# A residual stream through PSUM: where the sum between two phases is kept while the next norm reads it

## The reference, cut to what matters

```
def rms_norm(x, g):
    xf = x.astype(jnp.float32)
    y = xf * lax.rsqrt(jnp.mean(xf * xf, axis=-1, keepdims=True) + EPS)
    return (y * g.astype(jnp.float32)).astype(x.dtype)

# first block, twice
h = rms_norm(x, g_mix_norm[l]);  x = x + mix @ w_out[l]
h = rms_norm(x, g_ffn_norm[l]);  x = x + (silu(h @ w_gate[l]) * (h @ w_up[l])) @ w_down[l]

# second block, i = 0 (short convolution) and i = 1 (dilated attention)
h = h + mixed(rmsnorm(h, norm_mix[i]))
h = h + squared_relu_mlp(rmsnorm(h, norm_mlp[i]))
ple_gate = jax.nn.sigmoid(rmsnorm(h, norm_ple[i]) @ ple_w_gate[i])
h = h + ple_gate * (p[i] @ ple_w_proj[i])
return rmsnorm(h, norm_final)
```

## Time and profile before

| | us |
|---|---|
| median of 3 runs | 2726.02 |
| the profiled execution, whole | 2725.45 |
| its span | 2723.6 |
| TensorE busy | 2619.7 |
| GpSimd busy | 1665.5 |
| VectorE busy | 1270.6 |
| ScalarE busy | 471.2 |

### The profile page before, as it was taken

The page is one execution under the profiler, slowest core; times in us unless marked ns, Lnnn a source line. Parts: engine busy times, 40 slices in busy tenths (PEclk is TensorE's granted clock), DMA queues, the critical chain, the costliest instruction groups (busy, mean ns, idle before and its releaser), DMA issues.

```text
span 2723.6 us, 31500 instructions
## 1 busy us (share of the span) xinstructions
PE 2619.7 (96%) x11906; PEld 2146.2 (79%) x11906; DVE 1270.6 (47%) x1678; ACT 471.2 (17%) x777; POOL 1665.5 (61%) x1113
## 2 busy tenths in 40 slices
PE   7889999999899999999999999999999999999997
PEld 6668888877578888787888887788788878888885
DVE  5755443046654440345740514983367246604326
ACT  3332111023421110100100102300310042100012
POOL 5526677664276676666776766676347625767763
PEclk9899999999899999999999999999999999999998
DMA  4102222231022222222222222222112212232221
GB/s 151 62 16 93 100 100 93 94 113 62 16 93 96 104 92 93 93 93 93 101 97 103 92 93 101 91 95 93 63 47 92 100 40 70 93 108 93 93 92 62
DMA packets 36891, 236.70 MB, mean 87 GB/s; under 512 B 4048, under 2 KB 5584, under 8 KB 9168
## 3 DMA queue, kind: packets, MB, share of 16 engines
q1 hardware_dynamic: 33456, 230.78, 24.2%
q10 hardware_dynamic: 3360, 4.85, 0.5%
HBM read 233.51 MB, written 2.10 MB: 87 GB/s over the span
## 4 chain that ended last, share of the span: by engine, by line
PE 88%; DVE 7%; issue 2%; ACT 2%; POOL 0%; DMA 0%; DVEq 0%; SPq 0%; POOLq 0%; ACTq 0%
PE psum L457 27%; PE psum L458 27%; PE psum L459 27%; PE psum L906 2%; DVE work L1289 2%; DVE x_low L1303 1%; PE psum L890 1%; PE psum L668 1%; PE psum L915 1%; PE psum L778 1%; PE psum L794 0%; PE psum L487 0%; DMA x_res<-in_x 0%; DVE rstd L1296 0%; DVE work L1409 0%
## 5 line engine op out<-in xcount | busy, mean ns | idle before, releaser
L399 POOL TENSOR_TENSOR w_low<-w_stage,w_high 128x512 fp32r<-128x512 f32 x864 | 1214.4, 1436 | 18.0
L395 POOL TENSOR_SCALAR w_high<-w_stage 128x2048 fp32r<-128x2048 f32 x216 | 420.0, 1944 | 1004.8 <-PE psum L459 993.4
L457 PE MATMUL psum<-x_high,w_high 128*128 128x512 f32 x1664 | 654.5, 393 | 23.8 <-DVE x_low L1303 22.3
L458 PE MATMUL psum<-x_low,w_high 128*128 128x512 f32 x1664 | 648.7, 390 | 0.0
L459 PE MATMUL psum<-x_high,w_low 128*128 128x512 f32 x1664 | 648.6, 390 | 0.0
L457 PEld LDWEIGHTS psum<-x_high,w_high 128*128 128x128 f32 x1664 | 313.1, 188 | 94.9 <-issue 19.4
L458 PEld LDWEIGHTS psum<-x_low,w_high 128*128 128x128 f32 x1664 | 313.2, 188 | 67.2 <-issue 2.2
L459 PEld LDWEIGHTS psum<-x_high,w_low 128*128 128x128 f32 x1664 | 313.0, 188 | 65.3
L1329 DVE TENSOR_TENSOR x_res<-psum,x_res 128x512 f32<-128x512 f32 x64 | 47.0, 735 | 416.2 <-PE psum L459 416.2
L457 PE MATMUL psum<-mlp_high,w_high 128*128 (+1 forms) x576 | 225.5, 391 | 2.9 <-DVE mlp_low L1395 2.9
L458 PE MATMUL psum<-mlp_low,w_high 128*128 (+1 forms) x576 | 225.1, 391 | 0.0
(11 more groups left out here) (257 smaller groups left out, 3534.6 us busy)
## 6 DMA issues: line engine op xcount, KB each, us to landing
w_stage<-in_wstream SPq DMA_DIRECT2D x216, 1024.0 KB, 4.9
x_res<-in_x SPq DMA_DIRECT2D x2, 1024.0 KB, 11.7
out_x<-attn_out SPq DMA_DIRECT2D x8, 256.0 KB, 2.1
inv_count_sb<-in_inv_count ACTq DMA_DIRECT2D x2, 512.0 KB, 8.7
ple_proj<-in_p ACTq DMA_DIRECT2D x2, 512.0 KB, 3.7
qk<-in_mask ACTq DMA_DIRECT2D x1, 576.0 KB, 3.9
w_spat<-in_spatial ACTq DMA_DIRECT2D x2, 256.0 KB, 5.3
diag_sb<-in_diag ACTq DMA_DIRECT2D x2, 256.0 KB, 9.4
```

The source lines that it names most:

```text
L395: pool.tensor_scalar(wh[:, s, :], stage[:, s, :], 1.0, 1.0, ALU.mult, ALU.mult).then_inc(high_written, 1)
L399: last = pool.tensor_tensor(wl[:, s, part], stage[:, s, part], wh[:, s, part].bitcast(F32), ALU.subtract)
L457: pe.matmul(out, wa, ra, start=start, stop=False)
L458: pe.matmul(out, wa, rb, start=False, stop=False)
```

## The change

In all borders but the last one the sum of bank and x is written back **into the PSUM bank**. A new semaphore `x_summed` tells ScalarE of it. ScalarE copies the bank to x and makes the high part from the bank (`keep_sum`); VectorE makes x_low from the bank (`low_of_sum`); when that is done ScalarE squares the bank in place (`square_sum`), and VectorE adds the square from there to the running sum (`accumulate_sum`). Only then is the bank released. VectorE's order becomes: add of tile m, low of tile m-1, square-add of tile m-2. The gate's chain of ple (scale, sigmoid, product, sum) stays in the bank too, with a new semaphore `gate_scaled`. Before the final norm the gate's sum still goes to x and the squares to SBUF. In front of attn the bank is read with a step of four; behind attn the bank is read in a row, and x, high, low and the running sum are addressed with a step of four.

```diff
--- before.py
+++ after.py
...
@@ -357,6 +361,14 @@
             if p.kind == "attn":
                 return by_class(dst, False), by_class(x[:, m, :], True)
             return dst, x[:, m, :]
+
+        def summed_tile(p, before, m):
+
+            if before.kind == "attn":
+                return by_class(ps[:, m, :], False), lambda dst: by_class(dst, True)
+            if p.kind == "attn":
+                return by_class(ps[:, m, :], True), lambda dst: by_class(dst, False)
+            return ps[:, m, :], lambda dst: dst
 
         block = ctx.enter_context(nc.Block())
 
@@ -980,18 +992,41 @@
                 added[0] += 1
                 reader[n % 2] = (squares_added, added[0])
 
-            def scale_tile(p, m):
-                dst, src = operand(p, high_of(p, m), m)
-                act.activation(dst, src, ACT.Copy, scale=gcol(p.gain + m)).then_inc(x_scaled, 1)
-
-            def open_norm(p, ready, first):
+            def open_norm(p, before, first_square):
 
                 for m in range(DT):
-                    act.wait_ge(*ready[m])
-                    if p.kind != "final" and (m >= first or p.kind != "attn"):
-                        scale_tile(p, m)
-                    if m >= first:
+                    act.wait_ge(*x_ready(p, before, m))
+                    if p.kind != "final":
+                        act.activation(xh[:, m, :], x[:, m, :], ACT.Copy, scale=gcol(p.gain + m)).then_inc(x_scaled, 1)
+                    if m >= first_square:
                         norm_square(p, m)
+
+            def keep_sum(p, before, m):
+
+                act.wait_ge(*x_ready(p, before, m))
+                src, order = summed_tile(p, before, m)
+                if before.kind == "attn":
+                    act.activation(by_class(x[:, m, :], True), src, ACT.Copy)
+                else:
+                    act.activation(x[:, m, :], ps[:, m, :], ACT.Copy)
+                act.activation(order(high_of(p, m)), src, ACT.Copy, scale=gcol(p.gain + m)).then_inc(x_scaled, 1)
+
+            def square_sum(p, m):
+
+                act.wait_ge(x_low, 8 * p.norm + m + 1)
+                act.activation(ps[:, m, :], ps[:, m, :], ACT.Square).then_inc(squares_ready, 1)
+                n = state["sq"]
+                state["sq"] += 1
+                added[0] += 1
+                reader[n % 2] = (squares_added, added[0])
+
+            def open_psum_norm(p, before):
+
+                for m in range(DT + 1):
+                    if m < DT:
+                        keep_sum(p, before, m)
+                    if m >= 1:
+                        square_sum(p, m - 1)
 
             def split_tile(dst, src, scale=1.0):
                 act.activation(dst, src, ACT.Copy, scale=scale).then_inc(split_high, 1)
...
@@ -1051,10 +1084,16 @@
                     act.wait_ge(slab_done, p.slab)
                     load(mask_landing, a["mask2"])
                 for m in range(DT):
-                    act.wait_ge(drained[m], p.drain[m] + (2 if m < 7 else 3))
-                    act.activation(W[:, m % 2, :], W[:, m % 2, :], ACT.Sigmoid).then_inc(act_fn, 1)
-                    if m >= 2:
-                        next_square(m - 2)
+                    act.wait_ge(gate_scaled, DT * p.layer + m + 1)
+                    act.activation(ps[:, m, :], ps[:, m, :], ACT.Sigmoid).then_inc(act_fn, 1)
+                    if following.kind == "final":
+                        if m >= 2:
+                            next_square(m - 2)
+                    else:
+                        if m >= 1:
+                            keep_sum(following, p, m - 1)
+                        if m >= 2:
+                            square_sum(following, m - 2)
 
             def mix_loads(p):
                 L = p.layer
...
@@ -1296,38 +1342,65 @@
                 dve.reciprocal(dst, W[:, ROOT, :]).then_inc(rstd_ready, 1)
                 dve.wait_ge(rstd_ready, state["sums"])
 
-            def low(p, m):
-                dve.wait_ge(x_scaled, 8 * p.norm + m + 1)
-                dst, src = operand(p, low_of(p, m), m)
-                high, _ = operand(p, high_of(p, m).bitcast(F32), m)
-                dve.scalar_tensor_tensor(out=dst, in0=src, scalar=gcol(p.gain + m), in1=high,
-                                         op0=ALU.mult, op1=ALU.subtract).then_inc(x_low, 1)
-
-            def open_norm(p, residual, first):
+            def open_norm(p, first):
 
                 for m in range(DT + 1):
-                    if m < DT and residual:
-                        residual(m)
                     if m >= 1:
-                        if p.kind != "final" and (m > first or p.kind != "attn"):
-                            low(p, m - 1)
+                        if p.kind != "final":
+                            dve.wait_ge(x_scaled, 8 * p.norm + m)
+                            dve.scalar_tensor_tensor(out=xl[:, m - 1, :], in0=x[:, m - 1, :], scalar=gcol(p.gain + m - 1),
+                                                     in1=xh[:, m - 1, :].bitcast(F32), op0=ALU.mult, op1=ALU.subtract) \
+                                .then_inc(x_low, 1)
                         if m > first:
                             accumulate(m == 1)
                 state["acc_sum"] = state["sums"] + 1
+                finish_norm(p)
+
+            def low_of_sum(p, before, m):
+
+                dve.wait_ge(x_scaled, 8 * p.norm + m + 1)
+                src, order = summed_tile(p, before, m)
+                dve.scalar_tensor_tensor(out=order(low_of(p, m)), in0=src, scalar=gcol(p.gain + m),
+                                         in1=order(high_of(p, m).bitcast(F32)), op0=ALU.mult, op1=ALU.subtract).then_inc(x_low, 1)
+
+            def accumulate_sum(p, before, m):
+
+                n, k = state["sq"], state["added"]
+                dve.wait_ge(squares_ready, n + 1)
+                src, order = summed_tile(p, before, m)
+                acc = order(W[:, ACC, :])
+                if m == 0:
+                    at_least(dve, summed, state["acc_sum"])
+                    dve.tensor_copy(acc, src).then_inc(squares_added, 1)
+                else:
+                    tt(acc, acc, src, ALU.add).then_inc(squares_added, 1)
+                dve.wait_ge(squares_added, k + 1)
+                dve.sem_inc(drained[m], 1)
+                state["sq"] += 1
+                state["added"] += 1
+
+            def open_psum_norm(p, before):
+
+                signals = last_results(before)
+                for m in range(DT + 2):
+                    if m < DT:
+                        dve.wait_ge(*signals[m])
+                        if before.kind == "attn":
+                            flat = by_class(ps[:, m, :], False)
+                            tt(flat, flat, by_class(x[:, m, :], True), ALU.add).then_inc(x_summed, 1)
+                        else:
+                            tt(ps[:, m, :], ps[:, m, :], x[:, m, :], ALU.add).then_inc(x_summed, 1)
+                    if 1 <= m <= DT:
+                        low_of_sum(p, before, m - 1)
+                    if m >= 2:
+                        accumulate_sum(p, before, m - 2)
+                state["acc_sum"] = state["sums"] + 1
                 if p.kind != "ple":
                     finish_norm(p)
 
             def finish_norm(p):
                 dve.wait_ge(drained[7], p.drain[7] + (2 if p.kind == "ple" else 1))
                 reciprocal(rstd[:])
-
-            def add_from_psum(p):
-                signals = last_results(p)
-                def residual(m):
-                    dve.wait_ge(*signals[m])
-                    src, dst = operand(p, ps[:, m, :], m)
-                    tt(dst, src, dst, ALU.add).then_inc(drained[m], 1)
-                return residual
 
             def ffn(p):
                 with dve.Fori(0, FFN_TILES // 2) as i:
@@ -1402,17 +1475,25 @@
                 for m in range(DT + 1):
                     if m < DT:
                         dve.wait_ge(*tile_end(run, m))
-                        tt(W[:, m % 2, :], ps[:, m, :], rstd[:], ALU.mult).then_inc(drained[m], 1)
+                        tt(ps[:, m, :], ps[:, m, :], rstd[:], ALU.mult).then_inc(gate_scaled, 1)
                     if m >= 1:
                         k = m - 1
                         dve.wait_ge(act_fn, fn0 + k + 1)
-                        step(tt(W[:, k % 2, :], W[:, k % 2, :], pj[:, k, :], ALU.mult))
-                        tt(x[:, k, :], x[:, k, :], W[:, k % 2, :], ALU.add).then_inc(x_updated, 1)
-                        dve.wait_ge(x_updated, DT * p.layer + k + 1)
-                    if 2 <= m < DT:
-                        if following.kind == "attn":
-                            low(following, m - 2)
-                        accumulate(m == 2)
+                        step(tt(ps[:, k, :], ps[:, k, :], pj[:, k, :], ALU.mult))
+                        if following.kind == "final":
+                            tt(x[:, k, :], ps[:, k, :], x[:, k, :], ALU.add).then_inc(x_updated, 1)
```

(47 more changed lines are left out.)

## The result

| | us |
|---|---|
| before, median of 4 runs beside the changed kernel | 2725.07 (2722.59 to 2730.25) |
| after, median of 4 runs | 2700.55 (2695.03 to 2703.81) |
| ratio, 95% interval | 0.9906 [0.9895, 0.9918] |
| profiled execution, before and after | 2725.45 and 2697.78 |

A forecast was written before the change was run, and what follows sets the result against it. TensorE is busy 96%, so only its gaps, from late VectorE operations with two SBUF inputs beside GpSimd's splits, can be won: 7.0 + 4.9 + 7.1 + 2.6 + 3.4 = 25.0 us, median 2701, range 2697 to 2714.

The forecast's parts named there:

- Borders to mix and conv: Down projection to mix and to conv: VectorE at 2.06 a tile leaves TensorE no wait, gain 3.55 + 3.49 = 7.0 us.
- ple projections: Down projection to ple, twice: gain 2.42 + 2.49 = 4.9 us; banks held until the square-add, closest cover 1.1 us.
- ple to attention: First attention slab after ple's gate: 18.13 falls to 10.98, gain 7.1 us, taking strided PSUM reads at 1.13.
- Rival C: Strided PSUM reads take 2 us: attention's part turns from +7.1 to -1.3, total 2710; chance 0.06.
- Writes to PSUM: VectorE or ScalarE operations writing PSUM, not shown in the trace: taken at 0.69 us, bounds 0.67 and 1.13.
- Rival A: PSUM writes or handovers cost some tenths, 0.85 an operation in all: total 2709 to 2713; chance 0.15.
- the estimate by the errata section of the Trainium skill: PSUM sources cost 0.06 us more per VectorE operation, making the summed gain 1.5 us smaller.
- Mix output projection: Both mix output projections: w_low wait falls from 3.25 to 1.9, gain 2.6 us, plus 3.4 or 0 from the clock.
- conv: Border after conv's output projection: only the last tile counts, nothing lost now and nothing after.
- The final norm: Behind the last matmul: same operations in the same order, GpSimd idle, gain 0.
- at the borders: Borders to mix and conv, to ple, and to attention together: 7.0 + 4.9 + 7.1 = 19.0 us.

The follow-up runs named there:

- experiment 3: Kernel before, all operands in SBUF, only VectorE's order changed (square-add one tile later): 2720.78 us, ratio 0.9981.
- experiment 1: Kernel before with GpSimd's low split of the weights cut to 32 of every 512 columns from the third slab on: 2686.88 us, ratio 0.9854.
- experiment 6: Changed kernel with one more VectorE operation a tile, a copy of the square, between square-add and bank release: 2717.98 us, ratio 0.9973.
- experiment 7: Changed kernel with ScalarE's new copy made twice per tile, not at the border behind attention: 2705.5 us, ratio 0.9931.
- experiments 5 and 9: 5: changed kernel, gate chain and norm before attention back in SBUF, 2703.96 us. 9: changed kernel, conv's chain also kept in PSUM banks, 2693.41 us.
- changed kernel's second profile: The changed kernel run again unaltered, on the chip of two later kernels: 2696.47 us, ratio 0.9897.

## Why the prediction was right, step by step

- *Borders to mix and conv*, forecast 3.55 + 3.49, measured 14.43 - 10.88 and 14.37 - 10.88, the same two numbers. VectorE's pace came out as worked. Its queue at the border to mix (start, duration, operation):

```profile
578.06 0.70 DVE L1392 TENSOR_TENSOR psum<-psum,x_res 128x512 f32<-128x512 f32 x1
578.67 0.74 DVE L1363 SCALAR_TENSOR_TENSOR x_low<-psum,cols_sb,x_high 128x512 fp32r<-128x512 f32 x1
579.33 0.68 DVE L1376 TENSOR_TENSOR work<-work,psum 128x512 f32<-128x512 f32 x1
...
580.15 0.70 DVE L1392 TENSOR_TENSOR psum<-psum,x_res 128x512 f32<-128x512 f32 x1
```

  From add to add 2.09, where the forecast had 2.06. The step from square-add to add, 0.82, is longer than the other two, since VectorE first waits for the square-add's end to release the bank; the forecast had no term for that. The cause was half stated: the new order alone would bring 3.3 of these 7.0 (experiment 3), and short durations alone all of them (experiment 1). The forecast's queues were run with both; the text named the durations only.
- *ple projections*, forecast 2.42 + 2.49, measured the same in TensorE's stretch, and 2.52 and 2.61 to the norm's sum, because the late first gate matmul went too (0.1 each). The cover was as thin as said: one more VectorE operation a tile turns it into a loss (experiment 6), and one more ScalarE operation costs 1.6 each (experiment 7).
- *ple to attention*, forecast 7.1, measured 7.25. The result held with a wrong size in it. I took 1.13 and 1.2 for strided reads of PSUM; the trace has 0.68 for ScalarE's (above) and, by form, for VectorE's:

```profile
L1363 DVE SCALAR_TENSOR_TENSOR attn_x_low<-psum,cols_sb,attn_x_high 128x512 fp32r<-128x512 f32 x8 | 5.9, 742 | 0.1
```

  Even at 1.13 only 0.1 of wait was left to win, so the error cost nothing. Rival C has no ground. The note on cachelines in the Trainium skill (SBUF — State Buffer) says that non-contiguous access to PSUM slows matmuls; of VectorE and ScalarE it says nothing. For these two the step of four in PSUM is free here (0.742 and 0.683), and the same step in SBUF is not (1.126 at the least and 1.219).
- *Writes to PSUM*, the cost that no row of before showed: taken at 0.69, measured 0.700 (L1392). Rival A, 0.85 an operation, falls with it, and so does the estimate by the errata section of the Trainium skill (VectorE: DVE Perf Modes): 0.700 with PSUM on both sides is not 0.06 above the 0.691 of SBUF operands beside a quiet GpSimd.
- *Mix output projection*, forecast 2.6 for the waits and 3.4 for the clock, together 6.0, measured 5.8 in the profiled pair. The wait is 1.88, forecast 1.9, and the second is 3.7 - 1.88 = 1.8. The clock's share is less firm than this looks. Both waits of 3.2 were followed by a stretch at a granted clock of 0.50 in the kernel before and in that of experiment 3; of the two in the changed kernel's first profile neither was, but in its second the wait of 1.87 was (0.50 from 194 to 196 us). Over all profiles here it followed four of four waits of 3.2, and three of fourteen of 1.8 to 2.1: rarer behind the shorter wait, not gone. In the four profiled executions that share the changed kernel's code in mix (its two, and those of experiments 5 and 9) the two stretches together take 382.3 to 389.0, the first alone 193.5 to 196.4, against 393.2 in the one of before; and the kernel of experiment 3, whose norm in mix differs from before only in VectorE's order, has 399.0. Much of the spread of the changed kernel's single runs, 2694 to 2704, is probably this: those under 2698 have a mean granted clock of 0.985 or 0.986, those above 2701 one of 0.982 to 0.984.
- *conv* was missed: 2.8 gained, forecast 0. Its wait for the low part is about as long as before (2.84 against 2.85), but in the kernel before a stretch at half clock followed and in this execution none did. The windows behind the wait, in the kernel before and then in the changed one (stretch; us; busy time of PE, PEld, DVE, ACT, POOL; granted clock; DMA; GB/s):

```profile
1284.00:1288.00 4.00, 4.00 (x11) 3.11 (x10) 1.03 (x2) 1.24 (x2) 0.12 (x1) 0.50 0.04 14
```

```profile
1271.00:1275.00 4.00, 4.00 (x19) 3.28 (x18) 2.05 (x3) 2.49 (x5) 1.83 (x1) 1.00 0.10 37
```

  0.50 is 1.2 GHz. In the changed kernel's second profile the wait is 2.85, the clock behind it 0.50 (1273 to 1275 us), and conv takes 179.64. In the other kernels that keep this wait conv takes 178.1 to 179.8, and 178.1 also in that of experiment 3, whose residual sums are all in SBUF: the half clock there comes and goes by the execution, and I don't count the 2.8 as the change's.
- *The final norm*, forecast 0, measured -0.4. The gate's last sum goes to x there, and the next square-add comes behind it, first in the kernel before, then in the changed one:

```profile
2705.02 0.69 DVE L1410 TENSOR_TENSOR x_res<-x_res,work 128x512 f32<-128x512 f32 x1
2705.74 0.69 DVE L1289 TENSOR_TENSOR work<-work 128x512 f32<-128x512 f32 x1
```

```profile
2676.95 0.69 DVE L1484 TENSOR_TENSOR x_res<-psum,x_res 128x512 f32<-128x512 f32 x1
2677.86 0.69 DVE L1335 TENSOR_TENSOR work<-work 128x512 f32<-128x512 f32 x1 [0.22 <-DVE x_res L1484]
```

  Both kernels wait for the add's own end. New is the increment of `drained` behind that wait, which releases the bank: 0.22 of idle time where 0.03 was, twice behind the last matmul.

Measured by stretch: 19.4 at the borders (forecast 19.0), 5.8 in mix (6.0), 2.8 and -0.4 not forecast, 0.1 in attn: 27.7. Between the medians it was 24.5 in the first comparison (2725.07 - 2700.55) and 27.7 in the second (2724.15 - 2696.47). That the first median met the forecast to 0.5 is partly luck: the second lies 4.5 under it, just below the 2697 to 2707 that the forecast claimed by itself, and the clock behind the waits, which I can't foretell, moves a run by several us.

What stays open: why the half clock follows one wait of 2.85 and not another as long. No run here sets it apart.

## What to carry to other kernels

Where GpSimd works beside VectorE all the time, look at the minimum against the median of each VectorE operation: a wide gap on those with both inputs in SBUF and none on those with one in PSUM says that a PSUM operand will bring the minimum back, and the minimum is a good price for the forecast. Work the queues through in their new order, and try the order alone too: it was a fifth of this gain for four lines. When a bank is held longer for it, find the consumer that wants banks soonest (here the ple projection), for that is where the gain turns first.

## What the runs showed of the hardware

- VectorE beside GpSimd: a square-add of 128x512 with both inputs in SBUF takes 0.673 to 0.694 beside an idle GpSimd and 1.668 to 1.779 beside its low split. With one input in PSUM the median is 0.677 though GpSimd is as busy. GpSimd loses as well: its four low pieces take 6.4 beside the first kind and 5.0 beside the second.
- In-place operations in PSUM are not dearer: VectorE 0.700 for an add (0.691 in SBUF, in the median beside a quiet GpSimd), ScalarE 0.601 for a square (0.616 from SBUF to SBUF).
- A step of four elements costs nothing on reads from PSUM (0.742 and 0.683) and 0.4 to 0.5 on reads from SBUF (1.126 at the least, 1.219).
